# A two-layer decoder on one core: in the mLSTM heads, where the wait for a store stands, how the next head's weights are split, and when its inputs are rounded

## The reference, cut to what matters

```
q = einsum('bthd,hde->bhte', ca_h, w_q)
k = einsum('bthd,hde->bhte', ca_h, w_k) * DH_C ** -0.5
v = einsum('bthd,hde->bhte', xm.reshape(B, T, H_C, DH_C), w_v)
# each chunk, with weights from the gates:
s = einsum('bhtd,bhsd->bhts', q, k) * exp(d - m_t)
num = w_inter * einsum('bhtd,bhde->bhte', q, C) + einsum('bhts,bhse->bhte', s, v)
C_new = decay * C + einsum('bhsd,bhse->bhde', k * w_s, v)
```

## Time and profile before

| what | us |
|---|---|
| median of 3 runs | 2199.07 |
| lowest and highest of them | 2183.91, 2199.4 |
| profiled execution, whole | 2197.43 |
| its span, first to last instruction | 2195.7 |
| TensorE busy, mean granted clock | 1993.1, 0.955 |
| heads: first value tile to last chunk | 1219.9 to 1962 |

### The profile page before, as it was taken

The page is one execution under the profiler, slowest core; times in us unless marked ns, Lnnn a source line. Parts: engine busy times, 40 slices in busy tenths (PEclk is TensorE's granted clock), DMA queues, the critical chain, the costliest instruction groups (busy, mean ns, idle before and its releaser), DMA issues. The chain is left out here.

```text
span 2195.7 us, 28418 instructions
## 1 busy us (share of the span) xinstructions
PE 1993.1 (91%) x11413; PEld 1634.6 (74%) x11413; DVE 1121.5 (51%) x1815; ACT 674.5 (31%) x1185; POOL 118.4 (5%) x195
## 2 busy tenths in 40 slices
PE   5999998787776989999999899899999999989998
PEld 4999996555544869999999685595586568555886
DVE  5242113888433435544434557756845875675542
ACT  4211112777322224322222422321231232134321
POOL 0000000000221000000000001101100110100000
PEclk9999998999897999999999999999997999989999
DMA  4111113200676224765693425624551662757542
GB/s 155 39 42 57 53 40 97 60 2 1 214 230 217 74 56 89 124 155 121 159 206 118 164 77 192 196 79 162 185 167 68 206 201 64 220 184 252 184 153 87
DMA packets 174647, 282.67 MB, mean 129 GB/s; under 512 B 15683, under 2 KB 110727, under 8 KB 173402
## 3 DMA queue, kind: packets, MB, share of 16 engines
q1 hardware_dynamic: 146533, 179.54, 29.1%
q0 software_dynamic: 27840, 100.80, 14.0%
q10 hardware_dynamic: 144, 0.52, 0.1%
HBM read 185.70 MB, written 95.31 MB: 128 GB/s over the span
## 5 line engine op out<-in xcount | busy, mean ns | idle before, releaser
L1445 PE MATMUL pre_ps<-x_xh,pre_wh 128*128 128x358 f32 (+1 forms) x792 | 259.7, 328 | 6.7 <-DVE pre_wl L1567 6.7
L1446 PE MATMUL pre_ps<-norm_xl,pre_wh 128*128 128x358 f32 (+1 forms) x792 | 258.2, 326 | 0.0
L1447 PE MATMUL pre_ps<-x_xh,pre_wl 128*128 128x358 f32 (+1 forms) x792 | 257.5, 325 | 0.0
L426 PE MATMUL proj_ps<-x_xe,proj_wh 128*128 128x368 f32 x480 | 160.8, 335 | 4.8 <-DVE proj_wl L539 4.8
L428 PE MATMUL proj_ps<-x_xe,proj_wl 128*128 128x368 f32 x480 | 159.3, 332 | 0.0
L427 PE MATMUL proj_ps<-lo_xl,proj_wh 128*128 128x368 f32 x480 | 158.9, 331 | 0.0
L1445 PEld LDWEIGHTS pre_ps<-x_xh,pre_wh 128*128 128x128 f32 x792 | 149.3, 189 | 8.2 <-DVE pre_wl L1567 7.2
L1447 PEld LDWEIGHTS pre_ps<-x_xh,pre_wl 128*128 128x128 f32 x792 | 149.4, 189 | 0.0
L1446 PEld LDWEIGHTS pre_ps<-norm_xl,pre_wh 128*128 128x128 f32 x792 | 149.3, 188 | 0.0
L539 DVE TENSOR_TENSOR proj_wl<-all_w,proj_wh 128x1024 fp32r<-128x1024 f32 x24 | 29.2, 1225 | 192.7 <-ACT proj_wh L501 192.7
L1911 PE MATMUL head_ps<-head_cl,head_wh 128*128 128x358 f32 (+1 forms) x384 | 125.3, 326 | 0.0
(11 more groups left out here) (443 smaller groups left out, 4284.8 us busy)
## 6 DMA issues: line engine op xcount, KB each, us to landing
head_Cs<-in_state_C POOLq DMA_DIRECT2D x20, 1024.0 KB, 8.9
out_C_s<-head_Cs POOLq DMA_DIRECT2D x19, 1024.0 KB, 5.1
x_xnT<-in_cache_sb_k SPq DMA_DIRECT2D x64, 256.0 KB, 3.2
all_w<-in_w_in_c SPq DMA_DIRECT2D x32, 512.0 KB, 9.2
all_w<-in_w_in_a SPq DMA_DIRECT2D x24, 512.0 KB, 3.9
paged_vp<-in_cache_sb_v POOLq DMA_DIRECT2D x48, 256.0 KB, 4.4
head_Cs_top<-in_state_C POOLq DMA_DIRECT2D x12, 1024.0 KB, 8.9
out_C_s<-head_Cs_top POOLq DMA_DIRECT2D x12, 1024.0 KB, 4.7
```

The costliest lines, as they stand in the source:

```text
L426: pe.matmul(out, wh[:, t % 2, k, :], xh[:, k, c0:c1], start=(k == 0), stop=False)
L1445: pe.matmul(out, wh[:, t % 2, k, :], xh[:, k, c0:c1], start=(k == 0), stop=False)
L1446: pe.matmul(out, wh[:, t % 2, k, :], xl[:, k, c0:c1], start=False, stop=False)
L1447: last = pe.matmul(out, wl[:, t % 2, k, :], xh[:, k, c0:c1], start=False, stop=(k == KD - 1))
```

## The change

ACT still waits for `c_in` before quarter 0 of `ch`, but for `c_out` only before quarter 2, the first that lies over C. The quarters move from n = 4 to 7 to n = 5 to 8, on ACT and on DVE. The next head's w_k is split in two halves after chunks 3 and 4, and w_v in two halves after chunks 5 and 6; in head 0 w_k is split in two halves one after the other. In chunk 7 ACT makes `high_x(e + 1, 0)` ahead of `decayed`; DVE keeps `low_x(e + 1, 0)` where it was and makes `low_x(e + 1, 1)` after `prompt_states`. No DMA is added, and none changes its place in its queue. The diff, cut:

```
+        CH_OVER_C = 2
...
                 if n == 0 and e >= 1:
-                    pe.wait_ge(wlv, e)
+                    pe.wait_ge(wlv, 2 * e)
...
-                    pe.wait_ge(wlk, e + 1)
+                    pe.wait_ge(wlk, 2 * (e + 1))
...
             def high_c(e, k):
                 if k == 0:
                     act.wait_ge(c_in, 16 * (e + 1))
-                    if e >= 1:
-                        act.wait_ge(c_out, 16 * e)
+                if k == CH_OVER_C and e >= 1:
+                    act.wait_ge(c_out, 16 * e)
...
-                act.activation(wh[:, 0], w[:, 0], ACT.Copy).then_inc(whv, 1)
+                act.activation(wh[:, 0, halves(h)], w[:, 0, halves(h)], ACT.Copy).then_inc(whv, 1)
...
-                    if n >= KH and n < 2 * KH:
-                        high_c(e, n - KH)
+                    if n >= NV - KH:
+                        high_c(e, n - (NV - KH))
...
                     high_keys(e, c)
+                    if c == NT - 1 and e + 1 < HC:
+                        high_x(e + 1, 0)
                     decayed(e, c)
                     if e + 1 < HC:
-                        if c == 4:
-                            high_wk(e + 1)
-                        elif c == 6:
-                            high_wv(e + 1)
+                        if c in (3, 4):
+                            high_wk(e + 1, c - 3)
+                        elif c in (5, 6):
+                            high_wv(e + 1, c - 5)
...
                     if c == NT - 1 and e + 1 < HC:
                         low_x(e + 1, 0)
-                        low_x(e + 1, 1)
                     numerator(e, c)
                     prompt_states(e, c)
+                    if c == NT - 1 and e + 1 < HC:
+                        low_x(e + 1, 1)
                     moments(e, c)
-                        if c == 4:
-                            low_w(1, whk, wlk, e + 1)
-                        elif c == 6:
-                            low_w(0, whv, wlv, e)
+                        if c in (3, 4):
+                            low_half(1, whk, wlk, e + 1, c - 3)
+                        elif c in (5, 6):
+                            low_half(0, whv, wlv, e, c - 5)
```

More of the change, by code:

```diff
@@ L1732, in heads @@
         assert s.place["Cs"] + 8 * QM + 8 * XT <= s.place["ks"] and s.place["t1"] >= s.place["Cs"] + 8 * QM + 4 * XT
+        CH_OVER_C = 2
+        assert s.place["Cs"] + 4 * QM + 4 * XT * CH_OVER_C <= s.place["C"]
         ps = s.ps("ps", [P, 8, BANK])
@@ L1768, in heads, with halves @@
         LAST = B - 1
+        def halves(h):
+            return slice(KH // 2 * h, KH // 2 * (h + 1))
         def c_unit(c, m):
@@ L2109, in high_first, with high_wv, high_wk @@
                     act.activation(wh[:, 0, k, :], w[:, 0, k, :], ACT.Copy).then_inc(whv0, 1)
-            def high_wv(e):
+            def high_wv(e, h):
                 act.wait_ge(wv_in, 16 * (e + 1))
                 act.wait_ge(p_full, NJ * e)
-                act.activation(wh[:, 0], w[:, 0], ACT.Copy).then_inc(whv, 1)
-            def high_wk(e):
+                act.activation(wh[:, 0, halves(h)], w[:, 0, halves(h)], ACT.Copy).then_inc(whv, 1)
+            def high_wk(e, h):
                 act.wait_ge(wk_in, 16 * (e + 1))
@@ L2119, in high_wk @@
                     act.wait_ge(p_full, NJ * (e - 1) + KH)
-                act.activation(wh[:, 1], w[:, 1], ACT.Copy).then_inc(whk, 1)
+                act.activation(wh[:, 1, halves(h)], w[:, 1, halves(h)], ACT.Copy).then_inc(whk, 1)
             def high_wq(e):
@@ L2185, in _ @@
             for e in range(HC):
-                high_x(e, 0)
                 if e == 0:
+                    high_x(0, 0)
                     high_first()
@@ L2190, in _ @@
                 if e == 0:
-                    high_wk(0)
+                    high_wk(0, 0)
+                    high_wk(0, 1)
                 for n in range(NV):
@@ L2246, in low_w, with low_half @@
                 dve.tensor_tensor(wl[:, slot], w[:, slot], wh[:, slot].bitcast(F32), ALU.subtract).then_inc(done, 1)
+            def low_half(slot, high, done, e, h):
+                dve.wait_ge(high, 2 * e + h + 1)
+                dve.tensor_tensor(wl[:, slot, halves(h)], w[:, slot, halves(h)], wh[:, slot, halves(h)].bitcast(F32), ALU.subtract).then_inc(done, 1)
             def sample_values(e):
@@ L2424, in _ @@
                     low_x(e, 1)
-                    low_w(1, whk, wlk, 0)
+                    low_half(1, whk, wlk, 0, 0)
+                    low_half(1, whk, wlk, 0, 1)
                 for n in range(NV):
@@ L2428, in _ @@
                         low_x(e, n + 2)
-                    if n >= KH and n < 2 * KH:
-                        low_c(e, n - KH)
+                    if n >= NV - KH:
+                        low_c(e, n - (NV - KH))
                     low_v(e, n)
```

## The result

| | kernel before | changed kernel |
|---|---|---|
| median of 20 runs, us | 2194.07 | 2182.23 |
| lowest and highest, us | 2182.91, 2212.94 | 2175.47, 2195.21 |
| profiled execution, us | 2197.43 | 2181.89 |

The ratio is 0.9946, with a 95% interval from 0.9931 to 0.9961: 11.8 us less, between 8.6 and 15.1. The forecast was 2182.5 us, but from a median of three runs, 2199.07; over twenty runs the kernel before is 5 us faster than that. So the time came out as forecast, and the gain did not: 11.8 us where 16.6 were forecast. What follows is about that difference.

A forecast was written before the change was run, and what follows sets the result against it. TensorE's matmuls fill 91% of the span, so time comes only from its gaps or low clock. 5.5 + 3.8 + 12.9 - 1.4 - 4.2 = 16.6 us off 2197.43, plus 1.64 to the median: 2182.5 us; range 2170 to 2195.

The forecast's parts named there:

- Weights in halves: Chunks behind the weight splits: half low parts delay the state update within its slack, taking off 5.5 us over three heads.
- the slack of 0.92 us: State update behind a weight split: 1.83 us late, but TensorE lost only 0.91, having two state banks; 0.92 us is slack.
- Next inputs later: Chunk 7: TensorE's 1.49 us wait for DVE's update of C shrinks by 1.25 us per head, 3.8 us in all.
- The wait for C's store: Value stages of heads 1 to 3: moved to quarter 2, ACT's wait is hidden, making 12.9 us available.
- 12.9 us of loss: Value stages of heads 1 to 3: 7.5, 4.7 and 0.7 us over the 25.9 us each needs.
- Later quarters: Ahead of each head's first projection: a new gap of 0.35 us in four heads, costing 1.4 us.
- The load of cr: Quarter 0 of ch still waits for this load; C's store and one-word stores, issued ahead, delay it, costing 4.2 us.
- around T0 + 18: Assumed landing of the load of cr, T0 being the start of a head's first value tile; a 0.8 us wait.
- The term of 4.2 us: Value stages: cost of the late load of cr, put at 1.4 us a head in three heads.
- the rival of the small stores: Value stages: load of cr waits for the one-word stores, costing 15.6 us instead of 4.2; about 2194 us, chance 0.22.
- the slower rival: Value stages: load of cr becomes the bound, landing at T0 + 24 in three heads; 2211 us, chance 0.06.

The follow-up runs named there:

- e2: Changed kernel with POOL waiting for cr's landing between C's store and the one-word stores of n, nothing left out; median 2178.89 us, ratio 0.9932.
- e7: Changed kernel with the one-word stores behind cr's landing and the quarters of ch back at n = 4 to 7; median 2179.61 us, ratio 0.9934.
- e1: Changed kernel without the one-word stores of n in heads 0 to 2, so an output is left out; median 2182.66 us, ratio 0.9944.
- e3: Changed kernel with POOL's store of C held until SP has issued the load of cr; median 2182.59 us, ratio 0.994.
- e6: Changed kernel with the one-word stores behind cr's landing, run again beside the changed kernel on one chip; median 2178.55 us, ratio 0.9927.
- e8: Changed kernel with both waits back at quarter 0 and quarters at n = 4 to 7; median 2196.09 us, ratio 1.0008.
- e4: Kernel before with only the wait for C's store moved to quarter 2 and quarters at n = 5 to 8; median 2192.0 us, ratio 0.9989.

## Why the prediction was right, and where it was not

*Weights in halves: right.* Steps of 11.89 and 11.91 us became 10.97 to 11.00; the halves are free, as the slack of 0.92 us said: 5.5 us.

*Next inputs later: right.* 1.49 us became 0.16 in each of three heads, 4.0 us where 3.8 were forecast, and tile 1 wasn't held up by `denominators`. The two together are 9.5 us, and they make up most of the 11.8 measured.

*The wait for C's store: the mechanism right, the term too large.* At quarter 2 ACT never waited for it; the store had landed 9.6 us after its issue at the latest. But 12.9 us of loss to be had was one profile's number. Three more gave 9.3, 6.1 and 8.8 us (their sums less 3 x 25.9).

*Later quarters: right.* A gap of 0.24 to 0.31 us in heads 0, 2 and 3, for 0.35, and none in head 1.

*The load of cr: its lateness foreseen, its price not.* C's store came to stand 0.68 us ahead of the load, for "about 0.6"; the one-word stores came with the load, 0.08 us behind its issue, and not ahead of it. Landings "around T0 + 18" were 21.0, 18.6 and 19.5. The term of 4.2 us is best measured against e2, in which no load is late and the three stages take 80.3 us: 89.2 - 80.3 = 8.9 us in that profile, and 6.8 on average over three. This is the step that failed, together with the 12.9: I had set the value stages to gain 12.9 - 4.2 less the gaps; they gained 1.4 us from profile to profile, and nothing on average. Two small slips change nothing: in e7, where nothing waits, a stage takes 26.3 us, not 25.9; and a wait of 0.8 us, at the rate of 7.5 for 4.60, is 1.3 us a head and 3.9 in all, not 4.2.

Of the signs that I had named, the one for the rival of the small stores came: ACT idle at quarter 0 for `cr` until T0 + 21, and in head 1 a stage at a granted clock of 0.90. That the small stores hold the load back is what e1 and e2 show in every head. The way that the rival gave, a late count with the data already there, is seen in the kernel before; in the changed kernel the data was late. Its price was wrong too: 15.6 us, where 8.9 were lost, and 2194 in whole time, reckoned from the unusual profile and the high median.

So the forecast of 2182.5 is met by luck, by two errors that cancel: value stages some 7 us too good, and a start some 5 us too high. Of the slower rival no load met the condition, a landing behind T0 + 21.5, but head 1 came within 0.5 us of it.

*What stays open.* The kernels e1, e2, e3, e6 and e7 have value stages 5 to 10 us shorter together than the changed kernel's profiles. By their ratios, 0.9927 to 0.9944 against 0.9946 and 0.9944, they are 0 to 4 us faster in whole time, with some 5 us of uncertainty in each. The sum over the profiles says that most of the stages' gain is there and that long stretches of low clock hide it; that this explains the medians too wasn't shown. The small stores behind the load (e2, e6) are faster than the kernel before, by 15 and 16 us by their ratios; that they beat the changed kernel is shown for the stages only. Nor was it shown why, in one order of issue, the load takes 11 us in one head and 19 in another.

## What to carry to other kernels

When a wait is taken off, look at what stood beside it: here a load that had landed with it took its place at once. Edits that make an engine faster change the order in which DMAs of two queues are issued: here 1.4 us were enough to turn it around, and the load that the stage needs landed later. Where the order matters, fix it with a wait, as one line did in e2. And judge a stage by several profiles: its loss in the one that I read was 1.4 times the mean of four.

## What the runs showed of the hardware that was not expected

Four stores of 128 single words, 2 KB in all, lengthen a 2144 KB load of another queue: it takes 10.5 to 11.8 us with the stores issued behind its landing (e2, e6, e7) and 15.9 to 19.1 us with them issued along with it (the changed kernel's three profiles and e8). With them issued 1.4 us behind it, in the kernel before and e4, it took anything from 11.3 to 19.9 us. A 1 MB store in the same place doesn't do that: without the small ones, the load takes 11.0 to 13.1 us (e1). In 4 us with the small stores under way the DMA engines show as 0.76 busy at 93 GB/s, against 1.03 at 405 without them.

The clock granted to TensorE at one and the same place of the program, chunk 0, differs from head to head and from run to run, with 7 to 14 or with 24 us at the lower level for the same instructions. Between 10 and 24 us there lie some 6 us in time.
